# State-space loop of a hybrid decoder step: the causal mask as a TensorE product, the outer product and the spread of C on TensorE, the decay on ScalarE

## The reference

```python
# prompt, chunked; per head h of group g
decay = jnp.exp(jnp.where(causal, seg, -jnp.inf))        # seg = a_cs[l] - a_cs[s]
cb    = jnp.einsum('bclgn,bcsgn->bclsg', Cc, Bc)
y_diag = jnp.einsum('bclsg,bclsgh,bcsghp->bclghp', cb, decay, xdt)
y_off  = jnp.einsum('bclgn,bcghpn,bclgh->bclghp', Cc, s_in, jnp.exp(a_cs))
# sample step, per sequence: one step of the recurrence
#   s = s * exp(dt*A) + (x*dt) outer B ;  y = s . C
```

## Time and profile before

| | |
|---|---|
| median of three runs | 3042.57 us (3033.44 to 3047.91) |
| profiled execution, its own time | 3044.38 us |
| span of the profiled execution | 3042.5 us |
| TensorE busy | 2805.2 us, 92% |
| VectorE, ScalarE, GpSimd busy | 1166.6, 782.4, 121.6 us |
| granted TensorE clock, mean | 0.954 of full speed |
| preparation of the state-space part and chunk states | about 1155 to 1189 us |
| loop over heads and sample sequences | about 1188 to 1316 us |

### The profile page before, as it was taken

How to read it: one execution, slowest core, us unless ns; L and a number is a source line. 1 busy time by engine, 2 the same in 40 slices (tenths; PEclk the granted TensorE clock), 3 DMA queues, 4 the chain that set the end, 5 groups by cost and what they waited for, 6 DMA issues and landing times.

```text
span 3042.5 us, 50665 instructions
## 1 busy us (share of the span) xinstructions
PE 2805.2 (92%) x21103; PEld 2597.4 (85%) x21103; DVE 1166.6 (38%) x1734; ACT 782.4 (26%) x1174; POOL 121.6 (4%) x115
## 2 busy tenths in 40 slices
PE   4999999996899786669999999999999999999998
PEld 4549999996787433359989999999999999999998
DVE  2322222226686715763433333333333333333333
ACT  1223111114343310142322121222212222122233
POOL 0000000000000002401100000000000000000001
PEclk9999999997799896679999999999999999999999
DMA  5135323322002652222222222222232222222222
GB/s 195 57 112 167 97 90 90 96 74 76 1 1 85 214 201 67 73 90 91 92 83 90 90 92 92 91 90 90 90 96 90 90 90 91 95 90 90 92 91 87
DMA packets 251880, 287.14 MB, mean 94 GB/s; under 512 B 21549, under 2 KB 244139, under 8 KB 247814
## 3 DMA queue, kind: packets, MB, share of 16 engines
q1 hardware_dynamic: 249214, 239.99, 25.2%
q0 software_dynamic: 2592, 46.14, 3.9%
HBM read 273.68 MB, written 20.71 MB: 97 GB/s over the span
## 4 chain that ended last, share of the span: by engine, by line
PE 86%; DVE 7%; ACT 2%; DMA 2%; issue 2%; SPq 0%; POOL 0%; ACTq 0%; POOLq 0%; DVEq 0%
PE PS L610 68%; PE PS L382 4%; PE PS L1112 2%; PE PS L1100 1%; DMA seg_raw<-in_cache_kv_cmp,idx_c 1%; PE PS L1081 1%; DMA win_t<-kvs_tok 1%; PE PS L1082 1%; DVE c_tmp L1660 1%; PE PS L1365 1%; DVE seg_ord L464 1%; PE PS L368 1%; PE PS L1329 1%; DVE st_s L1896 1%; PE PS L1854 1%
## 5 line engine op out<-in xcount | busy, mean ns | idle before, releaser
L597 DVE TENSOR_TENSOR w_lo<-w_raw,w_hi 128x1024 fp32r<-128x1024 f32 (+1 forms) x388 | 460.3, 1190 | 1387.5 <-ACT w_hi L591 1386.5
L591 ACT ACTIVATE w_hi<-w_raw 128x1024 fp32r<-128x1024 f32 (+1 forms) x388 | 395.4, 1024 | 1500.9 <-PE PS L610 1500.9
L610 PE MATMUL PS<-h_hi,w_hi 128*128 128x260 f32 x3360 | 675.3, 282 | 7.4 <-DVE w_lo L597 5.1
L610 PE MATMUL PS<-h_lo,w_hi 128*128 128x260 f32 x3360 | 675.1, 282 | 0.0
L610 PE MATMUL PS<-h_hi,w_lo 128*128 128x260 f32 x3360 | 673.9, 282 | 0.0
L610 PEld LDWEIGHTS PS<-h_hi,w_hi 128*128 128x128 f32 x3360 | 516.4, 189 | 8.3 <-issue 7.5
L610 PEld LDWEIGHTS PS<-h_lo,w_hi 128*128 128x128 f32 x3360 | 519.1, 189 | 0.0
L610 PEld LDWEIGHTS PS<-h_hi,w_lo 128*128 128x128 f32 x3360 | 518.0, 189 | 0.0
L610 PE MATMUL PS<-u_hi,w_hi 128*128 128x260 f32 x2048 | 411.1, 282 | 8.4 <-DVE u_lo L2241 8.4
L610 PE MATMUL PS<-u_lo,w_hi 128*128 128x260 f32 x2048 | 410.5, 282 | 0.0
L610 PE MATMUL PS<-u_hi,w_lo 128*128 128x260 f32 x2048 | 409.9, 281 | 0.0
(11 more groups left out here) (384 smaller groups left out, 2470.7 us busy)
## 6 DMA issues: line engine op xcount, KB each, us to landing
w_raw<-in_w_up SPq DMA_DIRECT2D x256, 256.0 KB, 2.8
w_raw<-in_w_down SPq DMA_DIRECT2D x256, 256.0 KB, 2.9
w_raw<-in_w_in SPq DMA_DIRECT2D x160, 256.0 KB, 2.9
w_raw<-in_w_out SPq DMA_DIRECT2D x64, 256.0 KB, 3.1
out_kv_win_s<-in_state_kv_win SPq DMA_DIRECT2D x8, 1022.0 KB, 7.5
win_t<-in_state_kv_win SPq DMA_DIRECT2D x16, 448.0 KB
xtok<-in_x_prompt SPq DMA_DIRECT2D x4, 1024.0 KB, 9.3
x_r<-in_x_prompt SPq DMA_DIRECT2D x4, 1024.0 KB, 6.4
```

The costliest lines, as they stand in the source:

```text
L591: ins = e.activation(hi, raw, ACT.Copy)
L597: ins = e.tensor_tensor(lo, raw, hi.bitcast(F32), ALU.subtract)
L610: mm = e.matmul(PS[:, bank + 2 * m + h, 0:HN], w, x[:, k0 + k, h * HN:h * HN + HN], start=st and c == 0, stop=sp and c == 2)
```

## The change

The head loop:

- `lower` is gone. TensorE adds the mask itself: after the `ebc` exponential has read the spread bank, a product of `upper_r` (0 or -1e30) with four copies of the identity, both rounded to the fast float32 form, is added into that bank (`mask`). ScalarE then takes the exponential of each of the four pieces with the negated sum as a bias of its own (four instructions of 128 columns in place of one of 512).
- The exponential `ebc` and the product `ce` leave out the first 128 columns, which nothing reads.

The sample step:

- `step_diag`, `step_act`, the outer product on VectorE and the GpSimd decay are gone. GpSimd picks row b of the token-ordered x, B and C side (`bc_row`, 8 partitions of 512). TensorE forms the outer product in eight products of 128 columns with 8 contraction rows and spreads C with one of 256 columns (`step_pe`). ScalarE decays the state, eight pieces of 128 columns (`step_decay`). VectorE adds PSUM into the state and reads C from PSUM.
- The preparation gains the turning of the sample tokens: 1 transpose for dt, 8 for x, 4 for B and C, with their evacuations (`dta_s`, `xdt_s`, `bct`), and rounded copies of the mask and the identity.
- The first two spreads and the selector products (L1837) move ahead of the chunk states or between them.

The core of the diff:

```diff
             def ssd_pool
-                    s = st_s[:, b % 2]
-                    e.tensor_tensor(s, s, ddb[:, :, NB + b:NB + b + 1].to_broadcast([P, 8, DS]), ALU.mult)\
-                     .then_inc(e_dec, 1)
+                    if b >= 2:
+                        e.wait_ge(e_prod, b - 1)
+                    e.tensor_scalar(bc_row[b % 2][:], bct[:], ident[0:NB, b:b + 1], None, ALU.mult).then_inc(e_row, 1)
...
-                e.tensor_tensor(ce[:, h % HS], ebc[:, h % HS], xa[:, 10 + h // 8, 0:SEQ], ALU.mult).then_inc(h_ce, 1)
+                e.tensor_tensor(ce[:, h % HS, P:SEQ], ebc[:, h % HS, P:SEQ], xa[:, 10 + h // 8, P:SEQ],
+                                ALU.mult).then_inc(h_ce, 1)
...
             def ssd_dve
-            for h in range(HS - 1):
-                lower(h)
-            step_first(e, ch)
+            e.wait_ge(e_bc, 1)
+            e.tensor_copy(ddb[:].rearrange("p k x -> p (k x)"), PS[:, 7, 0:P]).then_inc(e_ddb, 1)
             for h in range(NH):
-                if h % 2 == 0:
-                    step_diag(e, h // 2)
-                    if h:
-                        step_read(e, h // 2 - 1)
+                if h and h % 2 == 0:
+                    step_read(e, h // 2 - 1)
                 e.wait_ge(h_dec, h + 1)
                 e.tensor_tensor(dec[:, h % HS], dec[:, h % HS], cbm[:, h // 8].rearrange("p c l -> p (c l)"),
                                 ALU.mult).then_inc(h_m, 1)
-                if h + HS - 1 < NH:
-                    lower(h + HS - 1)
                 if h % 2:
                     if h > 1:
                         pair_out(e, h // 2 - 1)
-                    step_state(e, ch, h // 2)
+                    step_state(e, h // 2)
...
             def ssd_act
+            def spread_exp(h):
+                e.wait_ge(h_bc, h + 1)
+                if h >= HS:
+                    e.wait_ge(h_ce, h + 1 - HS)
+                e.activation(ebc[:, h % HS, P:SEQ], PS[:, SPREAD_BANK[h % HS], P:SEQ], ACT.Exp).then_inc(h_ebc, 1)
+            spread_exp(0)
+            e.wait_ge(h_neg, 1)
+            for h in range(NH):
+                if h + 1 < NH:
+                    spread_exp(h + 1)
+                e.wait_ge(h_masked, h + 1)
+                if h >= HS:
+                    e.wait_ge(h_y, h + 1 - HS)
+                for c in range(NC):
+                    last = e.activation(dec[:, h % HS, c * P:c * P + P],
+                                        PS[:, SPREAD_BANK[h % HS], c * P:c * P + P], ACT.Exp,
+                                        bias=dta[:, c, 1, h:h + 1])
+                last.then_inc(h_dec, 1)
+                if h % 2 == 0:
+                    step_decay(e, h // 2)
...
             def ssd_pe
+            for f in range(2):
+                e.wait_ge(*d_xa(4 * f + 4))
+                for x in range(4):
+                    last = e.transpose(PS[0:NB, 2 + f % 2, x * P:x * P + P], xa[:, 4 * f + x, SEQ:NT], ident[:])
+                last.then_inc(d_xT.sem, 1)
...
+            def mask(h):
+                e.wait_ge(h_ebc, h + 1)
+                e.matmul(PS[:, SPREAD_BANK[h % HS], :], upper_r[:],
+                         ident_r[:].unsqueeze(1).to_broadcast([P, NC, P]), start=False, stop=True,
+                         skip_group_check=True).then_inc(h_masked, 1)
...
             for h in range(NH):
                 if h + HS - 1 < NH:
                     spread(h + HS - 1)
+                if h + 1 < NH:
+                    mask(h + 1)
                 if h % 2:
                     step_pe(e, h // 2)
...
         def step_pe(e, b):
-            e.wait_ge(e_diag, b + 1)
+            e.wait_ge(e_row, b + 1)
+            if b:
+                e.wait_ge(e_new, b)
+            else:
+                e.wait_ge(e_ddb, 1)
             if b >= 2:
-                e.wait_ge(e_bcs, b - 1)
-            e.matmul(PS[:, 2 + b % 2, :], ones[:], diag_b[:].rearrange("p x n -> p (x n)"), start=True,
-                     stop=True).then_inc(e_bc, 1)
+                e.wait_ge(e_rd, b - 1)
+            row = bc_row[b % 2]
+            for k in range(8):
+                e.matmul(PS[:, 2 + k // 4, (k % 4) * DS:(k % 4) * DS + DS], xdt_s[:, k * P:k * P + P],
+                         row[:, (k // 4) * DS:(k // 4) * DS + DS], start=True, stop=True)
+            e.matmul(PS[:, 7, (b % 2) * 256:(b % 2) * 256 + 256], ones[0:NB, :], row[:, 2 * DS:4 * DS],
+                     start=True, stop=True).then_inc(e_prod, 1)
+
+        def step_decay(e, b):
+            if b == 0:
+                e.wait_ge(e_ddb, 1)
+            e.wait_ge(e_ld[b % 2], 16 * (b // 2 + 1))
+            for k in range(8):
+                last = e.activation(st_s[:, b % 2, k, :], st_s[:, b % 2, k, :], ACT.Copy,
+                                    scale=ddb[:, k, NB + b:NB + b + 1])
+            last.then_inc(e_dec, 1)
+
+        def step_state(e, b):
             s = st_s[:, b % 2]
             e.wait_ge(e_dec, b + 1)
-            e.tensor_tensor(s, s, tmp_s[:], ALU.add).then_inc(e_new, 1)
+            e.wait_ge(e_prod, b + 1)
+            e.tensor_tensor(s, s, PS[:, 2:4, :].rearrange("p x (k n) -> p (x k) n", n=DS), ALU.add).then_inc(e_new, 1)
```

More of the change, by code:

```diff
@@ L1676, in ssd_dve @@
                             ALU.subtract).then_inc(d_ae.sem, 1)
+            e.wait_ge(*d_ae(1))
+            ch.settle()
+            e.tensor_scalar(dta[:, :, 1, :], dta[:, :, 1, :], -1.0, None, ALU.mult).then_inc(h_neg, 1)
+            for f in range(2 * NC, 2 * NC + 2):
+                half = f % 2
+                e.wait_ge(*d_xT(f - 2 * NC + 1))
+                e.tensor_tensor(xdt_s[:, half * 512:half * 512 + 512].rearrange("p (h d) -> p h d", d=HD),
+                                PS[0:NB, 2 + f % 2, :].rearrange("p (h d) -> p h d", d=HD),
+                                dta_s[:, 8 * half:8 * half + 8].unsqueeze(2).to_broadcast([NB, 8, HD]),
+                                ALU.mult).then_inc(d_xdt.sem, 1)
             for f in range(2 * NC):
                 c, half = f // 2, f % 2
-                e.wait_ge(*d_xT(f + 1))
+                e.wait_ge(*d_xT(f + 3))
                 e.tensor_tensor(xdt[:, c, half * 512:half * 512 + 512].rearrange("p (h d) -> p h d", d=HD),
@@ L1773, in ssd_act @@
                              ACT.Copy).then_inc(d_btok.sem, 1)
-            for h in range(NH):
-                e.wait_ge(h_min, h + 1)
+            e.wait_ge(*d_bT(3))
+            e.activation(bct[:], PS[0:NB, 4, :], ACT.Copy).then_inc(d_btok.sem, 1)
+            def spread_exp(h):
+                e.wait_ge(h_bc, h + 1)
                 if h >= HS:
                     e.wait_ge(h_ce, h + 1 - HS)
[L1778 to L1781, removed]
+                e.activation(ebc[:, h % HS, P:SEQ], PS[:, SPREAD_BANK[h % HS], P:SEQ], ACT.Exp).then_inc(h_ebc, 1)
[14 more added lines that the diff above has]
+                    step_decay(e, h // 2)
         def ssd_pe(e):
@@ L1788, in ssd_pe @@
                 last = e.transpose(PS[:, 0, c * 32 + 16:c * 32 + 32], acs[R, c * P:c * P + P], ident[R, R])
+            last = e.transpose(PS[0:NB, 0, P:P + NH], pt[R, T_GD, SEQ:NT], ident[R, R])
             last.then_inc(d_T.sem, 1)
@@ L1807, in ssd_pe @@
                 last.then_inc(d_bT.sem, 1)
+            e.wait_ge(*d_btok(1))
+            for x in range(4):
+                last = e.transpose(PS[0:NB, 4, x * P:x * P + P], xa[:, 8 + x, SEQ:NT], ident[:])
+            last.then_inc(d_bT.sem, 1)
             e.wait_ge(*d_xp(1))
@@ L1813, in ssd_pe, with spread @@
                 last.then_inc(d_cb.sem, 1)
+            def spread(h):
+                if h >= HS:
+                    e.wait_ge(h_dec, h + 1 - HS)
+                e.matmul(PS[:, SPREAD_BANK[h % HS], :], sel_h[R, h, :], acs[R, :], start=True, stop=True).then_inc(h_bc, 1)
+            def mask(h):
[3 more added lines that the diff above has]
+                         skip_group_check=True).then_inc(h_masked, 1)
+            e.wait_ge(d_selv, 2)
+            e.wait_ge(*d_ae(1))
+            for h in range(HS - 1):
+                spread(h)
             e.wait_ge(*d_btok(2))
-            e.wait_ge(*d_xdt(2 * NC))
+            e.wait_ge(*d_xdt(2 * NC + 2))
             for c in range(NC):
@@ L1822, in ssd_pe @@
                              start=True, stop=True).then_inc(d_st.sem, 1)
[L1824 to L1838, removed]
+                if c == 0:
+                    e.wait_ge(*e_dd(1))
+                    e.wait_ge(*d_cbm(2))
+                    for k in range(8):
+                        last = e.matmul(PS[:, 7, 16 * k:16 * k + 16], sel_p[R, k, :], dd[R, :], start=True, stop=True)
+                    last.then_inc(e_bc, 1)
+                if c == 1:
+                    mask(0)
             for h in range(NH):
@@ L1917, in ssd_end_pe @@
             e.wait_ge(d_stc, 2 * NC)
[L1918 removed]
+            e.wait_ge(h_dec, NH)
             for k in range(8):
@@ L1923, in ssd_end_pe @@
             e.wait_ge(h_out, 8)
+            e.wait_ge(e_new, NB)
```

72 lines of the change are left out of this document (22 added, 50 removed).

## The result

The changed kernel takes 3005.95 us as the median of four runs (2998.63 to 3013.24), against 3042.39 us (3033.44 to 3047.91) for four of the kernel before: a ratio of 0.9893, 95% interval 0.9862 to 0.9923. The forecast was 3012 us, 2994 to 3032. The profiled execution took 3005.51 us.

A forecast was written before the change was run, and what follows sets the result against it. A chain of waits through the state-space loop, VectorE and TensorE by turns, was taken as the bound. Loop 25.0 plus start 10.0 minus preparation 4.3 gave 30.7 us off 3044.4, less 1.8: 3012 us, range 2994 to 3032.

The forecast's parts named there:

- the clock stays near 0.7: Sign of a wrong prediction: TensorE's granted clock in the head loop near 0.7, where over 0.9 was expected.
- Period: Head loop, one sequence and two heads: 14.57 us falls to 11.0, gaining 25.0 us over seven periods.
- serial cycle: Head loop: read, m, y, spread, mask, step_pe, addition and handovers follow one another, 10.3 us at full clock.
- the row at 81% busy: Profile row, 1020 to 1060 us: TensorE busy 32.25 of 40 us at clock 1.00; the new loop was said to resemble it.
- TensorE becomes the bound: Rival, head loop: at the lower clock the period is 15.7 us, kernel 5.4 us slower, 3048 us; chance 0.10.
- the clock swings: Rival "half of it", head loop: period 12 to 14.5 us, gain 13.3 us at 13, kernel 3029 us; chance 0.13.
- Start: From the end of the chunk states to the first new state: 21.0 us falls to 11, gaining 10.0 us.
- Preparation: Before and between the chunk states: added transposes and moved small products cost 4.3 us, between 2.9 and 6.1.
- more than forecast: Case: period 10.3, start 8.2, preparation 2.9, gain 40.0 us, 3002.6 us, or 2996 with faster chunk products; chance 0.17.
- a rival needed 0.61: Rival, head loop: ScalarE binds if an activation piece costs over 0.61 us; about 3029 us at 0.74; chance 0.05.
- new(b): Head loop: VectorE's addition into a sample state takes 1.24 us, with 2.17 as the other bound.
- Tail: After new(7), the last sample state: read, pair_out and last small products as before, no change.

The follow-up runs named there:

- step over 128 rows: The changed kernel with the outer product and spread of C contracting over 128 rows (120 zeros) instead of 8; not faster, period 11.96 us.
- both over 128 rows: The changed kernel with the step's products and the spread of acs all contracting over 128 rows, zero-filled; 2992.65 us, 0.9843 of the kernel before.
- wide, sample-step half alone: The changed kernel with all those products over 128 rows and the mask half undone (`lower` on VectorE, one exponential of 512 columns); 2999.97 us.

## Why the prediction was right

The total was right (3012 forecast, 3005.95 measured), and the gain does come from the loop and its start. But the mechanism of the period was not the one forecast, one of the prediction's own signs of being wrong came true ("the clock stays near 0.7"), and the total owes part of its closeness to terms that cancel: the loop gained 6.3 us less than forecast (18.7 against 25.0), the preparation 6.8 more, the start 2.6 more, the tail 2.6 more, and 2.3 came from outside the state-space part. That they met within 6 us is luck.

- **Period: 11.0 forecast, 11.9 measured.** The serial cycle was summed rightly: 10.3 us at full clock, and 10.00 us where the clock is 1.00 and TensorE waits. But in the changed kernel this cycle does not set the period. The forecast had gaps before y of an even head; TensorE had 1 us of idle time in the whole loop. The step that failed is the clock. The prediction took over 0.9, from the row at 81% busy; measured was 0.71. TensorE's own work, 8.5 us per pair at full clock, over 0.71 gives 12.0 us: the period. The rivals "TensorE becomes the bound" and "the clock swings" had the right picture together. Their times (3048 and 3029) came out too high: the second took a period of 13 us (7.7 us of the difference), and the start and preparation of the lower clock (4.2 and 8.6 us). In size, the mask is the other miss: 0.43 us in the chain above at full clock, against 0.3.
- **Why the row misled.** It was read by busy share, and the loops were compared by that. What told them apart is the kind of product: with narrow ones the clock fell at 99% busy, without them it stayed at 79% busy with gaps of 2 us. That the rows count is shown by the runs with zeros in them: "step over 128 rows" and "both over 128 rows" have the same queue and like gaps (1.77 to 2.39 and 1.98 to 2.39 us), and differ on TensorE in the rows of the spread alone, with 0.84 and 1.00 of the clock. The Trainium skill, "TensorE: Matmul & The Clock Gate", section "HAM oscillation — how this bites in real kernels", puts the swings down to idle gaps. In the change they came without any, so gaps are not the cause there. Gaps are no rival that is ruled out, though: "wide, sample-step half alone" agrees with the Trainium skill, with three falls at gaps of 1.98 to 2.82 us and no narrow product, and in "step over 128 rows" the falls came behind a gap and a 16-row spread together.
- **Start: 11 forecast, 8.4 measured** (8.2 was the sum at full clock), 10.9 in the other profile of the change. Granted were 0.85 and 0.66. In the first, all parts but the spread of C have their full-clock length. The forecast lies above both; what decides the clock there is open.
- **Preparation: 4.3 us more forecast, 2.5 us less measured**, 0.7 us less in the other profile. The case "more than forecast" had the picture of the first: 0.89 of the clock from 1166.5 to 1182.5 against 0.59 near there before, and the last two pairs of chunk products at 1.98 us. But its reason, that the small products keep the clock up, is not shown: with them in place the second profile had pairs of 3.78 and 2.44 us, and with them moved back the stretch took 33.1 us, next to the 33.0 of that profile. What keeps the clock up there is open.
- **ScalarE: hidden, right.** 0.305 us a piece for the decays and 17.1 / 60 = 0.285 for the exponentials, against 0.368 taken; a rival needed 0.61. The Trainium skill, "ScalarE: Activation LUTs", section "What ACT_TABLE_LOAD costs", gave 0.29, and this trace agrees.
- **new(b): right.** 1.22 us from PSUM every time. `step_pe`'s products 2.0 us: right at full clock, and in the change they stand at full clock nearly always, with the fall at their end.
- **Tail: no change forecast, 2.6 us less measured.** It goes with the clock in that stretch: 26.8 us in six profiles, all with 0.88 to 0.94 granted from new(7) to the output projection, and 28.5 to 29.8 in the six others (the kernel before among them), with 0.79 to 0.85. Kernels with the new sample step stand on both sides, the two with the old one on the slow side, so the 2.6 us are not shown to be the change's. No run says what sets the clock there.
- **Slower than before** would have needed a period over 14.9 us. In none of the runs with the sample-step half was it over 12.95 us, at clocks down to 0.61.

The two halves were summed as one in the prediction, with the whole gain in one cycle. The runs show that the sample step's half carries it.

## What to carry to other kernels

Before small products are moved to an idle TensorE, look at how many contraction rows they use. If they stand in a loop that TensorE can bound, try the same products with the rows filled with zeros, and read the granted clock in stretches of 1 us, not only its mean. Try the order of the queue only after that: the same move lost 0.4% or more with narrow rows and shortened the period from 10.00 to 8.38 us with wide ones. And when a change has two halves, time each: here one of them carried the gain, and the other was worth 0.2% alone. One thing stays untested: the kernel before has 16-row spreads and 0.71 of the clock in its loop too, with idle gaps of some 6 us, and no run widened them there.

## What the runs showed of the hardware

- In the change the granted clock fell from 1.00 to 0.50 (2.4 to 1.2 GHz) while TensorE was without a gap: seven times in the products over 8 rows that follow a 16-row spread, once about 1 us behind them. It rose again at the end of stretches of y, over 128 rows, or just behind. With zeros up to 128 rows the mean over the loop went from 0.71 to 0.84 (step wide), 0.81 (spread wide) and 1.00 (both).
- Without any narrow product, in the wide kernel with the sample-step half alone, the clock fell three times in the loop, each time at or within 0.3 us behind an idle gap (1.98, 2.33 and 2.82 us); its mean was 0.93.
- A spread of 512 float32 columns and the mask behind it took 1.48 us with 16 contraction rows and 1.20 with 128, both at full clock.
- GpSimd took 1.55 us to scale 512 columns on 8 partitions (`bc_row`).
- The addition on VectorE took 1.22 us in all eight cases with its second operand in PSUM, six of them beside `bc_row`. Before, with both operands in SBUF, it took 2.17 us in the seven cases beside `ce` on 128 partitions and 1.24 in the one without. Both the operand and the neighbour changed, and no run parts the two.
